# Second block's MLP: the up product as seven products of sums, tokens as rows, in a ring of four slots

## What is computed

```python
h = rmsnorm(x, norm_mlp[l])                                            # 256 x 1024
hid = jnp.square(jax.nn.relu(jnp.einsum('bsd,df->bsf', h, w_up[l])))   # 256 x 4096
x = x + jnp.einsum('bsf,fd->bsd', hid, w_down[l])                      # 256 x 1024
return rmsnorm(x, norm_final)
```

## Time and profile before

| | before |
|---|---|
| median of 3 runs | 1817.99 us (1814.09 to 1819.8) |
| profiled execution | 1817.92 us, its span 1816.1 us |
| TensorE busy | 1684.5 us, 93% |
| VectorE busy | 547.5 us, 30% |
| ScalarE busy | 275.0 us, 15% |
| mean granted TensorE clock | 0.986 |

### The profile page before, as it was taken

The page is one execution under the profiler, slowest core; times in us unless marked ns, Lnnn a source line. Parts: engine busy times, 40 slices in busy tenths (PEclk is TensorE's granted clock), DMA queues, the critical chain, the costliest instruction groups (busy, mean ns, idle before and its releaser), DMA issues.

```text
span 1816.1 us, 18346 instructions
## 1 busy us (share of the span) xinstructions
PE 1684.5 (93%) x7208; PEld 893.4 (49%) x7208; DVE 547.5 (30%) x1067; ACT 275.0 (15%) x587; POOL 30.4 (2%) x33
## 2 busy tenths in 40 slices
PE   5999999999999798897988989988999999989998
PEld 3445686533332232332423323324767788578743
DVE  2333432333323232232232332323022221211355
ACT  3123450301010010100101001001242222010000
POOL 0110000000000000000000000001000000000000
PEclk9999999999999999999999999898999999989999
DMA  9785225899999999999999999999423233344320
GB/s 381 283 314 163 93 104 201 314 428 430 429 429 431 429 431 429 431 429 429 431 428 432 429 430 429 429 428 395 145 93 139 93 139 139 111 151 155 140 92 23
DMA packets 85529, 537.14 MB, mean 296 GB/s; under 512 B 6080, under 2 KB 7488, under 8 KB 59872
## 3 DMA queue, kind: packets, MB, share of 16 engines
q1 hardware_dynamic: 81664, 530.60, 72.1%
q10 hardware_dynamic: 3808, 5.78, 0.9%
HBM read 535.31 MB, written 1.05 MB: 295 GB/s over the span
## 4 chain that ended last, share of the span: by engine, by line
PE 72%; DMA 24%; DVE 1%; issue 1%; ACT 1%; DVEq 0%; ACTq 0%; SPq 0%; POOL 0%; POOLq 0%
PE ps L1555 33%; PE ps L1883 21%; DMA ring<-in_w_up 12%; DMA ring<-in_w_gate 10%; PE ps L2221 5%; PE ps L1863 3%; PE ps L1953 2%; DMA arena<-in_w_down 2%; DMA ring<-in_w_ada 1%; PE ps L1581 1%; PE ps L1744 1%; PE ps L1661 0%; PE ps L1696 0%; PE ps L1924 0%; PE ps L1719 0%
## 5 line engine op out<-in xcount | busy, mean ns | idle before, releaser
L1883 PE MATMUL ps<-ring,arena 128*64 128x512 f32 x2288 | 514.4, 598 | 55.7 <-DMA ring<-in_w_gate 28.0
L1555 PE MATMUL ps<-arena,ring 128*128 128x256 f32 x1856 | 414.1, 383 | 2.8 <-ACT arena L789 2.5
L1555 PEld LDWEIGHTS ps<-arena,ring 128*128 128x128 f32 x1856 | 354.1, 192 | 62.7 <-issue 7.1
L1883 PEld LDWEIGHTS ps<-ring,arena 128*64 128x64 f32 x2288 | 161.5, 137 | 390.4 <-issue 315.9
L1555 PE MATMUL ps<-ring,arena 128*128 128x512 f32 (+1 forms) x448 | 190.1, 579 | 1.8 <-issue 1.8
L1883 PE MATMUL ps<-arena 128*64 128x512 f32 x784 | 178.2, 600 | 10.0 <-DMA arena<-in_w_up 5.4
L1555 PEld LDWEIGHTS ps<-ring,arena 128*128 128x128 f32 x448 | 83.7, 190 | 99.9 <-issue 98.7
L746 ACT ACTIVATE arena<-ps 128x512 f32<-128x512 f32 x32 | 19.1, 597 | 671.2 <-PE ps L1924 671.2
L1883 PEld LDWEIGHTS ps<-arena 128*64 128x64 f32 x784 | 55.8, 138 | 118.1 <-issue 101.8
L1953 PE MATMUL ps<-arena 128*128 128x512 f32 x128 | 67.2, 657 | 20.8 <-DVE xres L1254 19.3
L1219 DVE TENSOR_TENSOR arena<-ps,arena 128x512 f32<-128x512 f32 x32 | 22.1, 691 | 204.8 <-PE ps L1883 204.8
(11 more groups left out here) (271 smaller groups left out, 1054.8 us busy)
## 6 DMA issues: line engine op xcount, KB each, us to landing
ring<-in_w_up SPq DMA_DIRECT2D x55, 2048.0 KB, 33.8
ring<-in_w_down SPq DMA_DIRECT2D x55, 2048.0 KB, 31.8
ring<-in_w_gate SPq DMA_DIRECT2D x49, 2048.0 KB, 33.6
ring<-in_w_in SPq DMA_DIRECT2D x23, 2048.0 KB, 9.2
arena<-in_w_up SPq DMA_DIRECT2D x17, 2048.0 KB, 29.7
arena<-in_w_down SPq DMA_DIRECT2D x17, 2048.0 KB, 32.0
arena<-in_w_gate SPq DMA_DIRECT2D x15, 2048.0 KB, 30.8
ring<-in_w_ada SPq DMA_DIRECT2D x12, 2048.0 KB, 17.3
```

The source lines that it names most:

```text
L1555: last = pe.matmul(dst, a, b, start=k == 0, stop=k == len(terms) - 1)
L1883: mm = pe.matmul(dst[CAP * g:CAP * g + CAP, :], stationary(half, c), w[:, c, 512 * g:512 * g + 512], start=half == 0 and c == 0, stop=half ...
```

## The change

The up stage takes the same form as the down stage. The 1024 features are cut into two halves, the 256 tokens into two tiles and the 512 columns of a block into two halves, so a block is a 2x2 by 2x2 product of quarters. Seven products replace eight. Each is four matmuls with 128 tokens as stationary and 256 columns of weights (or of sums of weights) as moving operand.

- VectorE makes three sums and one difference in place from each weight block (`weight_sums`, as single steps between its other work) and four sums of tokens once (`token_sums`).
- VectorE reads each product out of PSUM as it ends (`up_part`) and builds the four quarters in `upc`, with tokens as rows; relu and square are one instruction over 128x512.
- TensorE turns the block with eight 128x128 transposes (`up_turn`), after the second product of the next block; ScalarE copies the turned banks to `hid`.
- The first block's products 1 and 2 need token tile 0 alone and stand ahead of the transposes of token tile 1.
- The ring of the second block has RING2 = 4 slots; the other two (`spare`) hold the sums of tokens and weights.
- In the down stage the order of the products changes (`P_ORDER`), and the sums of tokens (`mlp_sums`) are made apart from those of the weights.

```diff
 CAP = 64
...
-            s = i % RING
+            s = i % RING if i < W_QKV2 else (W_QKV2 + (i - W_QKV2) % RING2) % RING
+            return ring[:, s * SLOT:(s + 1) * SLOT]
+
+        def spare(n):
+
+            s = (W_QKV2 + RING2 + n) % RING
             return ring[:, s * SLOT:(s + 1) * SLOT]
...
-        relu = area(14848, 1024).rearrange("p (b w) -> p b w", b=2)
+        upc = [area(a, 1024).rearrange("p (t n) -> p t n", t=TT) for a in (19968, 14848)]
+        upu, upv = area(20992, 256), area(21248, 256)
+        up_a = [spare(n // 2)[:, 3072 + 512 * (n % 2):3584 + 512 * (n % 2)].rearrange("p (j q) -> p j q", j=4)
+                for n in range(4)]
+
+        def up_b(i):
+
+            return [spare(i % 2)[:, 1024 * n:1024 * n + 1024].rearrange("p (j c) -> p j c", j=4) for n in range(3)]
+
+        UP_ORDER = [(1, 2, 4, 6, 5, 7, 3)] + 7 * [(1, 2, 6, 5, 7, 3, 4)]
+        UP_READ = [(1, 2, 6, 5, 7, 4, 3)] + 7 * [(1, 2, 6, 5, 7, 3, 4)]
+
+        def up_banks():
+
+            table, rest, last = {}, 0, {}
+            for i in range(8):
+                for n in UP_ORDER[i]:
+                    b = 4 if (i, n) == (0, 4) else rest % 4
+                    rest += b != 4
+                    table[i, n] = b, last.get(b, 0)
+                    last[b] = 7 * i + UP_READ[i].index(n) + 1
+            return table, last
+
+        UP_BANK, UP_LAST = up_banks()
         yout = area(17408, 2048).rearrange("p (t d) -> p t d", t=TT)
 
...
-        P_ORDER = (1, 2, 4, 3, 5, 6, 7)
+        P_ORDER = (1, 2, 5, 6, 7, 4, 3)
...
-                if j >= RING:
-                    sp_.wait_ge(used2, j - RING + 1)
+                if j >= RING2:
+                    sp_.wait_ge(used2, j - RING2 + 1)
                 elif j >= 0:
-                    s = j if j < 4 else j + 2
-                    last = s - MRING + 1 if s < MRING - 1 else -MRING
-                    sp_.wait_ge(block_used, passes[0] * (GROUPS * GROUP_BLOCKS) + (W_MOE + last + 1))
+                    sp_.wait_ge(block_used, passes[0] * (GROUPS * GROUP_BLOCKS) + (W_MOE + j - MRING + 2))
...
             for s in range(16):
-                act.wait_ge(sem("up2_done"), s + 1)
-                if s >= 2:
-                    act.wait_ge(sem("hid_done"), s - 1)
-                act.activation(relu[:, s % 2, :], bank(s % 4), ACT.Relu).then_inc(sem("up2_read"), 1)
+                act.wait_ge(sem("up2_turned"), s + 1)
+                act.activation(hid[:, 2 * s:2 * s + 2, :].rearrange("p j q -> p (j q)"), bank(4 + s % 4),
+                               ACT.Copy).then_inc(sem("hid_done"), 1)
...
+            def weight_sums(i, quarters, out):
+
+                (b11, b12, b21, b22), (t2, t3, t4) = quarters, out
+                j = i - W_QKV2
+                dve.wait_ge(loaded2[j % RING2], 16 * (j // RING2 + 1))
+                dve.tensor_tensor(t3, b22, b12, ALU.subtract)
+                dve.drain()
+                yield
+                dve.tensor_tensor(b12, b12, b11, ALU.subtract)
+                dve.drain()
+                yield
+                dve.tensor_tensor(t2, b22, b12, ALU.subtract)
+                dve.drain()
+                yield
+                dve.tensor_tensor(t4, t2, b21, ALU.subtract).then_inc(sem("sums_ready"), 1)
+                yield
+
+            def up_sums(i):
+                w = wq_view(W_UP2 + i)
+                return weight_sums(W_UP2 + i, (w[:, 0:4, 0:T], w[:, 0:4, T:2 * T], w[:, 4:8, 0:T], w[:, 4:8, T:2 * T]),
+                                   up_b(i))
+
+            def down_sums(i):
+                w = w4_view(W_DOWN2 + i)
+                return weight_sums(W_DOWN2 + i, (w[:, 0:2, 0:512], w[:, 0:2, 512:1024], w[:, 2:4, 0:512],
+                                                 w[:, 2:4, 512:1024]), quarter_sums(i)[1])
+
+            def token_sums(a11, a12, a21, a22, out):
+                s1, s2, s3, s4 = out
+                dve.drain()
+                dve.tensor_tensor(s1, a21, a22, ALU.add)
+                dve.drain()
+                dve.tensor_tensor(s2, s1, a11, ALU.subtract)
+                dve.drain()
+                dve.tensor_tensor(s3, a11, a21, ALU.subtract)
+                last = dve.tensor_tensor(s4, a12, s2, ALU.subtract)
+                return last
+
+            def mlp_sums(i):
+                dve.wait_ge(sem("hid_done"), 2 * i + 2)
+                token_sums(hid[:, 4 * i:4 * i + 2, 0:P], hid[:, 4 * i + 2:4 * i + 4, 0:P],
+                           hid[:, 4 * i:4 * i + 2, P:T], hid[:, 4 * i + 2:4 * i + 4, P:T],
+                           [quarter_sums(i)[0][:, n] for n in range(4)]).then_inc(sem("tokens_ready"), 1)
+
+            for step in up_sums(0):
+                pass
...
-                    down_sums((s - 11) // 2)
-            for i in range(2, 8):
-                dve.wait_ge(used2, W_DOWN2 - W_QKV2 + i - 1)
-                down_sums(i)
+            dve.wait_ge(sem("hy_act"), 2)
+            token_sums(hT2[:, 0:4, 0:P], hT2[:, 4:8, 0:P], hT2[:, 0:4, P:T], hT2[:, 4:8, P:T],
+                       up_a).then_inc(sem("tokens_ready"), 1)
+
+            def up_part(i, n):
+
+                c = upc[i % 2]
+                c11, c12, c21, c22 = c[:, 0, 0:T], c[:, 0, T:2 * T], c[:, 1, 0:T], c[:, 1, T:2 * T]
+                p = bank(UP_BANK[i, n][0], T)
+                dve.wait_ge(sem("up2_done"), 7 * i + UP_ORDER[i].index(n) + 1)
+                if n == 1:
+                    last = dve.tensor_copy(upu, p)
+                elif n == 2:
+                    if i >= 2:
+                        dve.wait_ge(sem("up2_turned"), 2 * (i - 1))
+                    last = dve.tensor_tensor(c11, p, upu, ALU.add)
+                elif n == 6:
+                    last = dve.tensor_tensor(upu, p, upu, ALU.add)
+                elif n == 5:
+                    last = dve.tensor_tensor(upv, p, upu, ALU.add)
+                elif n == 7:
+                    dve.tensor_tensor(c22, p, upv, ALU.add)
+                    last = dve.tensor_tensor(upu, p, upu, ALU.add)
+                elif n == 3:
+                    last = dve.tensor_tensor(c12, p, upv, ALU.add)
+                else:
+                    last = dve.tensor_tensor(c21, upu, p, ALU.subtract)
+                last.then_inc(sem("up2_read"), 1)
+                dve.drain()
+                if n in (3, 4):
+                    a = c[:, 0 if n == 3 else 1, :]
+                    last = dve.scalar_tensor_tensor(a, a, 0.0, a, ALU.max, ALU.mult)
+                    if n == UP_READ[i][6]:
+                        last.then_inc(sem("sq_done"), 1)
+
+            for i in range(8):
+                sums = up_sums(i + 1) if i < 7 else down_sums(0)
+                for n in UP_READ[i]:
+                    up_part(i, n)
+                    next(sums, None)
+                if i == 6:
+                    mlp_sums(0)
+            mlp_sums(1)
+            for i in range(1, 8):
+                if i >= 2:
+                    dve.wait_ge(used2, W_DOWN2 - W_QKV2 + i - 1)
+                    mlp_sums(i)
+                for step in down_sums(i):
+                    pass
...
-            norm_transpose(xn3, 1, "hy")
...
-            for s in range(16):
-                i = W_UP2 + s // 2
-                ready(i)
-                if s < 4:
-                    pe.wait_ge(sem("x3_done"), 4)
-                else:
-                    pe.wait_ge(sem("up2_read"), s - 3)
-                last = by_feature(bank(s % 4), wq_view(i), T * (s % 2), hT2, KC)
...
+
+            def up_product(i, n):
+                j0, tile, source = {1: (0, 0, None), 2: (4, 0, None), 3: (4, 1, up_a[3]), 4: (4, 1, None),
+                                    5: (0, 1, up_a[0]), 6: (0, 0, up_a[1]), 7: (0, 0, up_a[2])}[n]
+                w, (t2, t3, t4) = wq_view(W_UP2 + i), up_b(i)
+                b = {1: w[:, 0:4, 0:T], 2: w[:, 4:8, 0:T], 3: w[:, 4:8, T:2 * T], 4: t4, 5: w[:, 0:4, T:2 * T],
+                     6: t2, 7: t3}[n]
+                a = hT2[:, j0:j0 + 4, P * tile:P * tile + P] if source is None else source
+                at, free = UP_BANK[i, n]
+                if free:
+                    pe.wait_ge(sem("up2_read"), free)
+                product(bank(at, T), [(a[:, j, :], b[:, j, :]) for j in range(4)]).then_inc(sem("up2_done"), 1)
+
+            def up_turn(i):
+
+                pe.wait_ge(sem("sq_done"), i + 1)
+                if i >= 2:
+                    pe.wait_ge(sem("hid_done"), 2 * (i - 1))
+                for half in range(2):
+                    for c in range(2):
+                        for tt in range(TT):
+                            f = 2 * half + c
+                            last = pe.transpose(bank(4 + 2 * (i % 2) + half)[:, T * c + P * tt:T * c + P * tt + P],
+                                                upc[i % 2][:, tt, P * f:P * f + P], ident)
+                    last.then_inc(sem("up2_turned"), 1)
+
+            for i in range(8):
+                ready(W_UP2 + i)
+                for m, n in enumerate(UP_ORDER[i]):
```

(59 more changed lines are left out.)

## The result

The changed kernel takes 1803.82 us (median of 4 runs, 1802.39 to 1804.45), the kernel before 1818.8 us in the same comparison (4 runs, 1814.09 to 1819.8). The ratio is 0.9925, with a 95% interval of 0.9913 to 0.9938, so the change saves 11.3 to 15.8 us. The forecast was 1805 us, 13.0 less than before.

A forecast was written before the change was run, and what follows sets the result against it. TensorE alone was taken to bound the second block, so time saved in its up stage shortens the whole. 6.9 + 3.4 - 0.3 + 3.0 = 13.0 us off 1817.92 gave 1805 us, range 1801 to 1810.5.

The forecast's parts named there:

- The blocks: Up stage on TensorE: four matmuls fewer, eight transposes more, 13.82 to 12.96 us a block; 6.9 us gained over eight.
- The start: Output product to first turn: early products shorten TensorE's non-matmul time, 3.4 us gained, less 0.3 for VectorE's late square.
- The clock: Norm before the up stage: shorter TensorE pauses keep the clock from falling to half; 3.0 us gained.
- VectorE and the ring: Up stage: VectorE's added work (11.0 us of a 12.96 us block) and four-slot weight loads stay hidden; priced at nothing.
- The sum: Whole kernel: 6.9 + 3.4 - 0.3 + 3.0 = 13.0 us saved.

The follow-up runs named there:

- e3: Changed kernel with each transpose of the up stage's turns done twice, sixteen a turn in place of eight; 1810.56 us, ratio 0.9964.
- e4: Changed kernel with product 5 ahead of product 6 in the first up block, each behind its own token sum; 1801.31 us, ratio 0.9918.
- v1: Changed kernel with VectorE's first weight step done once more, behind a drain, in up blocks 1 to 7; 1807.52 us, ratio 0.995.
- e5: Kernel of e4 with the weight steps of up block 1 moved into VectorE's idle time around the norm; 1802.03 us, ratio 0.9925.
- e1: Changed kernel with the second tile's transposes and all hT2 waits again ahead of product 1 in the first up block; 1811.38 us, ratio 0.9967.
- before_again: The kernel before, unchanged, profiled a second time; 1817.04 us in its one run.
- e2: Kernel before with only the second block's ring changed, four slots in place of six; 1816.47 us, ratio 0.9997.

## Why the prediction was right

**The blocks** (forecast 6.9 us). A block was to go from 13.82 to 12.96 us; it is 12.96 from turn to turn, with transposes at 0.109 us each. e3 shows that the turn lies wholly on TensorE's path. The 275 ns that the Trainium skill gives, for bf16 (TensorE: Matmul & The Clock Gate, Part 4: PE-mode transpose), do not hold here as a price. They are near what one record lasts: the 64 transposes of the turns have records of 272 to 273 ns. The records overlap, and on the chain eight take 0.87 us. So a duration must not be read as what one more instruction costs.

**The start** (forecast 3.4 less 0.3). From the end of the output product to the first turn I had 19.31 us, and the trace has 19.46. That it comes so close is in part luck, since errors inside it cancel. TensorE's wait for the token sums is 0.91 us, not 1.2, and VectorE is not late at the first turn, where I had charged 0.3. On the other side, product 4 ends 7.92 us behind the output product (1588.85 to 1596.77, where the 0.91 us begin) and not 7.46, and the 24 matmuls behind the pause (16 of block 0, eight of block 1) take 10.63 us and not 10.37. Behind a pause a piece takes 0.2 to 0.3 us longer than one without: besides these 24, product 4 takes 1.96 us for 1.73, a turn 1.09 for 0.87 (e4, v1) and the 28 matmuls of e5 12.32 for 12.09. The sum had no term for this. Without the clock the start gave 2.9 us (6.83 - (19.46 - 36 x 0.432)) against 3.1 forecast, and e1 gives 3.0 for the order alone.

**The clock** (forecast 3.0, called the least certain). It stayed at 1.00, and e1 prices the fall at about 3.2 us. This was hardly chance: a low stretch of 10.2 us at this norm is in all four profiles without the early products (before, before_again, e1, e2), and none at this norm is in the six with them. What decides is what TensorE does during the norm, since e1 and the changed kernel differ in nothing else: e1 has a pause of 3.72 us there, the changed kernel none over 1.27. The same section of the Trainium skill says that transposes do not count as busy time for the clock gate in the same way. No run here tests this: the clock held with eight transposes, three pauses and the early products in the stretch, and in e1 it had fallen before its transposes began.

**VectorE and the ring** (priced at nothing). Both were hidden. I took VectorE's block for 9.7 us busy and 11.0 with its gaps; it is 9.5 and 10.2. The average gap was half of what I took: with a drain between two instructions it is 0.07 to 0.10 us, and without one the second starts some 0.08 us before the first has ended (1606.61 above, behind 0.69 us from 1606.00). Its spare time was 2.8 us a block and not 2, but only 0.5 in block 0, which e4 and v1 ran into. The ring of four changed nothing (e2, 216.50 against 216.55 us).

**The sum.** 13.0 us was forecast, and the stage gave 12.78. The two profiles differ by 15.5 in all; the 2.7 beyond the stage lie ahead of it, where the end of the output product wandered by 5.3 us over ten profiles. The timed saving, 11.3 to 15.8 us, includes the stage's figure; the 1803.8 us of the median came 1.2 under the forecast.

## What to carry to other kernels

Trading a product for sums on an idle engine pays by what TensorE itself gets in return: here four matmuls of 0.432 us against eight transposes of 0.109, and nearly half of the whole gain (5.9 of 12.8 us) came from elsewhere, from work that could be placed in a pause and from the clock that this kept up. A pause made short may also hand back the clock behind it, so ask what could run in each stretch in which TensorE waits for a norm. Ask for the helper engine's spare time block by block: the first block, where it starts late, had a fifth of that of the others, and there the next wait appeared as soon as the first was removed.

## What the runs showed of the hardware that was not expected

The stretch of low clock that follows a pause is not the same from run to run: at the norm around 1252 us, where all these programs run the same instructions on TensorE, it was 0, 3.4, 6.8 or 10.2 us long. At the second block's norm it was 10.2 us in all four profiles that had it.
